# Key numbers of a product-key search by XOR and minimum on 16-bit numbers

## The reference, cut to what matters

```python
q = jnp.einsum('bsd,dk->bsk', h, w_q).reshape(b, s, PEER_HEADS, 2, PEER_DHALF)
sc = jnp.einsum('bshpk,hpnk->bshpn', q, sub_keys).astype(jnp.float32)
s1, i1 = lax.top_k(sc[..., 0, :], PEER_TOPK)       # 16 of 128
s2, i2 = lax.top_k(sc[..., 1, :], PEER_TOPK)
cand = (s1[..., :, None] + s2[..., None, :]).reshape(b, s, PEER_HEADS, PEER_TOPK * PEER_TOPK)
cidx = (i1[..., :, None] * PEER_N_KEYS + i2[..., None, :]).reshape(b, s, PEER_HEADS, PEER_TOPK * PEER_TOPK)
top, pos = lax.top_k(cand, PEER_TOPK)              # 16 of 256
idx = jnp.take_along_axis(cidx, pos, axis=-1)
gate = jax.nn.softmax(top, axis=-1)
```

## Time and profile before

| | us |
|---|---|
| runs (3): median | 4100.17 |
| lowest, highest | 4097.18, 4105.68 |
| profiled execution | 4106.96 |
| its span, first to last instruction | 4105.1 |
| granted clock of TensorE, mean | 0.953 of full speed |

### The profile page before, as it was taken

How to read it: one execution, slowest core, us unless ns; L and a number is a source line. 1 busy time by engine, 2 the same in 40 slices (tenths; PEclk the granted TensorE clock), 3 DMA queues, 4 the chain that set the end, 5 groups by cost and what they waited for, 6 DMA issues and landing times.

```text
span 4105.1 us, 46071 instructions
## 1 busy us (share of the span) xinstructions
PE 3706.4 (90%) x14431; PEld 2467.1 (60%) x14431; DVE 2709.5 (66%) x5504; ACT 1238.0 (30%) x2640; POOL 1580.5 (39%) x1341
## 2 busy tenths in 40 slices
PE   6999989898888979867769899798999999999998
PEld 5778768677777768656434454453544545445763
DVE  1445542348778866666999989889876868743540
ACT  1333332232333232225342240330422404224530
POOL 2556534331222147655344443443454444410000
PEclk8999999899999989988889999899999999999999
DMA  7666633347766658878899999999999999963557
GB/s 237 203 223 218 211 103 93 97 157 238 233 220 222 219 177 262 275 237 313 315 362 391 361 391 368 353 388 356 381 402 393 406 404 394 398 266 125 185 199 275
DMA packets 506183, 1133.96 MB, mean 276 GB/s; under 512 B 41036, under 2 KB 250364, under 8 KB 505760
## 3 DMA queue, kind: packets, MB, share of 16 engines
q1 hardware_dynamic: 334976, 570.93, 40.2%
q0 software_dynamic: 147456, 536.94, 35.0%
q10 hardware_dynamic: 23584, 24.12, 1.7%
HBM read 1044.80 MB, written 89.41 MB: 276 GB/s over the span
## 4 chain that ended last, share of the span: by engine, by line
PE 34%; DVE 14%; DMA 3%; issue 2%; ACT 1%; POOL 0%; DVEq 0%; ACTq 0%; SPq 0%
PE ps L1390 27%; DVE u_ring L2399 6%; PE ps L1376 4%; PE ps L1422 2%; DMA u_ring<-in_peer_u,pidx 1%; DMA v_ring<-in_peer_v 1%; DVE split_v L2446 1%; ACT split_v L1846 1%; DVE hot L2391 1%; DVE hot L2392 1%; DVE pick_own L2002 0%; DVE pick_own L1997 0%; DVE got_own L2005 0%; PE h_up L1365 0%; DVE inds_own L1960 0%
## 5 line engine op out<-in xcount | busy, mean ns | idle before, releaser
L1390 PE MATMUL ps<-v_ring,table 128*128 128x512 f32 x3584 | 1593.1, 596 | 16.6 <-DMA v_ring<-in_peer_v 16.6
L993 POOL DMA_INDIRECT u_ring<-in_peer_u,pidx x800 | 772.1, 965 | 969.8 <-DVE coefe L2399 902.0
L1390 PEld LDWEIGHTS ps<-v_ring,table 128*128 128x128 f32 x3584 | 664.1, 191 | 772.2 <-issue 723.7
L2399 DVE CUSTOM_DVE_ANT_0 u_ring<-u_ring,h_up 128x1024 f32<-128x1024 f32 x800 | 948.1, 1218 | 140.4 <-DMA u_ring<-in_peer_u,pidx 125.1
L1052 PE MATMUL ps<-x_hi,w_hi 128*128 128x512 f32 x1280 | 516.1, 403 | 39.7 <-ACT w_hi L1498 23.6
L1055 PE MATMUL ps<-x_lo,w_hi 128*128 128x512 f32 x1280 | 506.0, 395 | 0.0
L937 POOL TENSOR_TENSOR w_lo<-w_raw,w_hi 128x1024 fp32r<-128x1024 f32 x120 | 302.1, 2522 | 196.5 <-ACT w_hi L1498 190.7
L1376 PEld LDWEIGHTS ps<-hot,hot 128*128 128x128 f32 x2048 | 282.0, 203 | 155.2 <-issue 112.6
L1814 ACT ACTIVATE table<-ps 128x512 f32<-128x512 f32 (+3 forms) x256 | 229.5, 896 | 438.4 <-PE ps L1376 391.7
L958 POOL DMA_INDIRECT e_ring<-in_peer_u,icole x224 | 233.7, 1043 | 290.4 <-DVE dotse L2057 210.9
L1802 ACT ACTIVATE hot<-hot,by_slot 128x128 f32<-128x128 f32 x1024 | 322.3, 389 | 73.4 <-DVE hot L2391 51.6
(11 more groups left out here) (332 smaller groups left out, 4266.5 us busy)
## 6 DMA issues: line engine op xcount, KB each, us to landing
v_ring<-in_peer_v SPq DMA_DIRECT2D x576, 512.0 KB
w_raw<-in_w_in SPq DMA_DIRECT2D x88, 512.0 KB
wh_d<-w_hi SPq DMA_DIRECT2D x56, 512.0 KB, 2.7
wl_d<-w_lo SPq DMA_DIRECT2D x56, 512.0 KB, 4.2
w_hi<-wh_d SPq DMA_DIRECT2D x56, 512.0 KB
w_lo<-wl_d SPq DMA_DIRECT2D x56, 512.0 KB
u_ring<-in_peer_u,pidx POOLq DMA_INDIRECT x800
raw_mid<-in_w_branch SPq DMA_DIRECT2D x48, 256.0 KB
```

The lines of the kernel that those rows point to most:

```text
L993: pool.indirect_dma_start(out=u_ring[:, slot_of(n, k), :], out_offset=None, in_=u_tab, in_offset=bass.IndirectOffsetOnAxis(ap=pidx[n % 2][ ...
L1390: last = pe.matmul(ps[2 * (n % 2) + c][:, :], table[:, row_of(n, i1), :], v_ring[:, j % V_TILES, HALF * c:HALF * c + HALF], start=(n == p ...
L2399: dve.tensor_tensor_reduce(out=u_ring[:, slot_of(n, k), :], in0=u_ring[:, slot_of(n, k), :], in1=h1_up[:, :, :].rearrange("p c n -> p (c n)"),
```

## The change

In part 1 the indices are no longer converted: 128 times the place (0 to 15) is added to them, with a constant `steps` that is loaded at the start, into 16-bit numbers `indk`. In part 3 the position's high and low four bits are shifted to the same place (times 128) and written twice each into `own`. The XOR of `indk` and `own` is the index alone, under 128, where the places agree, and 128 or more elsewhere; so the minimum along the 16 is the wanted index. The conversion `posf`, the comparison and the product go. `pick`, `indk` and `own` are 16-bit tiles at the places of the tiles before them; `steps` takes 64 bytes per partition ahead of most other tiles.

```diff
+        "c_steps": np.tile(np.arange(TOPK, dtype=np.uint32) * P, (P, 1)),
...
+        steps = at("steps", [P, TOPK], U32)
...
+            sp.dma_start(steps[:, :], A["c_steps"]).then_inc(const_in, 16)
...
-            pe.wait_ge(const_in, 176)
+            pe.wait_ge(const_in, 192)
...
-            dve.wait_ge(const_in, 176)
+            dve.wait_ge(const_in, 192)
...
-                    dve.tensor_copy(tk.indf[:, :, :], tk.inds[:, :, :]).then_inc(*mark("indf"))
+                    dve.tensor_tensor(out=tk.indk[:, :, :], in0=tk.inds[:, :, :], in1=steps[:, :].unsqueeze(1).to_broadcast([P, 4, TOPK]),
+                                      op=ALU.add).then_inc(*mark("indf"))
...
-                    dve.tensor_scalar(out=tk.posu[:, :, 0, :], in0=tk.pos[:, :, :], scalar1=4, scalar2=None, op0=ALU.logical_shift_right).then_inc(*mark("pos1_"))
-                    dve.tensor_scalar(out=tk.posu[:, :, 1, :], in0=tk.pos[:, :, :], scalar1=TOPK - 1, scalar2=None, op0=ALU.bitwise_and).then_inc(*mark("pos2_"))
-                    md("pos2_")
-                    dve.tensor_copy(tk.posf[:, :, :, :], tk.posu[:, :, :, :]).then_inc(*mark("posf"))
-                    md("posf")
-
-                    dve.tensor_tensor(out=tk.pick[:, :, :], in0=tk.iota[:, :].unsqueeze(1).to_broadcast([P, 4 * TOPK, TOPK]),
-                                      in1=tk.posf[:, :, :, :].rearrange("p h t k -> p (h t k)").unsqueeze(2).to_broadcast([P, 4 * TOPK, TOPK]),
-                                      op=ALU.is_equal).then_inc(*mark("eq"))
-                    md("eq")
-                    pk = tk.pick[:, :, :].rearrange("p (m k) c -> p m k c", m=4)
-                    dve.tensor_tensor(out=pk, in0=pk, in1=tk.indf[:, :, :].unsqueeze(2).to_broadcast([P, 4, TOPK, TOPK]),
-                                      op=ALU.mult).then_inc(*mark("in"))
-                    md("in")
-                    dve.tensor_reduce(out=tk.got[:, :, :, :].rearrange("p h t k -> p (h t k)"), in_=tk.pick[:, :, :], axis=AX, op=ALU.add).then_inc(*mark("got"))
+                    places = tk.pos[:, :, :].bitcast(U16).rearrange("p h (k w) -> p h k w", w=2)[:, :, :, 0:1].to_broadcast([P, 2, TOPK, 2])
+                    dve.tensor_scalar(out=tk.own[:, :, 0, :, :], in0=places, scalar1=TOPK * (TOPK - 1), scalar2=3,
+                                      op0=ALU.bitwise_and, op1=ALU.logical_shift_left).then_inc(*mark("own1_"))
+                    dve.tensor_scalar(out=tk.own[:, :, 1, :, :], in0=places, scalar1=TOPK - 1, scalar2=7,
+                                      op0=ALU.bitwise_and, op1=ALU.logical_shift_left).then_inc(*mark("own2_"))
+                    md("own2_")
+
+                    four = [P, 4, TOPK, TOPK // 2, 2]
+                    dve.tensor_tensor(out=tk.pick[:, :, :].rearrange("p (m k) (c u) -> p m k c u", m=4, u=2),
+                                      in0=tk.indk[:, :, :].unsqueeze(2).to_broadcast([P, 4, TOPK, TOPK]).rearrange("p m k (c u) -> p m k c u", u=2),
+                                      in1=tk.own[:, :, :, :, :].rearrange("p h t k u -> p (h t) k u").unsqueeze(3).to_broadcast(four),
+                                      op=ALU.bitwise_xor).then_inc(*mark("off"))
+                    md("off")
+                    dve.tensor_reduce(out=tk.got[:, :, :, :].rearrange("p h t k -> p (h t k)"), in_=tk.pick[:, :, :], axis=AX, op=ALU.min).then_inc(*mark("got"))
```

More of the change, by code:

```diff
@@ L30 @@
 U32 = mybir.dt.uint32
+U16 = mybir.dt.uint16
 ALU = mybir.AluOpType
@@ L317, in layer @@
         inds_side = at("inds_side", [P, 4, TOPK], U32)
-        indf_side = at("indf_side", [P, 4, TOPK])
+        at("indf_side", [P, 4, TOPK])
         got_side = at("got_side", [P, 2, 2, TOPK])
@@ L356, in early_topk_tiles @@
             t.cleft = at("cleft_all", [P, 2, TOPK * TOPK])
-            t.pick = at("pick_all", [P, 4 * TOPK, TOPK], offset=where["ptp1"] + 2048)
-            t.iota = keys[:, 0:TOPK]
+            t.pick = nc.alloc_sbuf_tensor_at("pick_all", [P, 4 * TOPK, TOPK], U16, offset=where["ptp1"] + 2048)
             t.vals = at("vals_all", [P, 4, TOPK], offset=where["chain"] + 2048)
             t.inds = at("inds_all", [P, 4, TOPK], U32)
-            t.indf = at("indf_all", [P, 4, TOPK])
-            t.posu = at("posu_all", [P, 2, 2, TOPK], U32)
-            t.posf = at("posf_all", [P, 2, 2, TOPK])
+            at("indf_all", [P, 4, TOPK])
+            t.indk = nc.alloc_sbuf_tensor_at("indk_all", [P, 4, TOPK], U16, offset=where["indf_all"])
+            at("own_all_", [P, 2, 2, TOPK])
+            t.own = nc.alloc_sbuf_tensor_at("own_all", [P, 2, 2, TOPK, 2], U16, offset=where["own_all_"])
             t.got = at("got_all", [P, 2, 2, TOPK])
@@ L377, in side_topk_tiles @@
             t.cleft = at("cleft_side", [P, 2, TOPK * TOPK])
[L378 to L381, removed]
+            t.pick = nc.alloc_sbuf_tensor_at("pick_side", [P, 4 * TOPK, TOPK], U16, offset=where["w_raw1"])
+            t.vals, t.got, t.best, t.pos = vals_side, got_side, best_side, pos_side
+            t.indk = nc.alloc_sbuf_tensor_at("indk_side", [P, 4, TOPK], U16, offset=where["indf_side"])
             t.inds = inds_side
-            t.posu = at("posu_side", [P, 2, 2, TOPK], U32, offset=where["inds_side"])
+            t.own = nc.alloc_sbuf_tensor_at("own_side", [P, 2, 2, TOPK, 2], U16, offset=where["inds_side"])
             return t
@@ L449, in late_topk_tiles @@
             t.cleft = lay("cleft", "hot1_1", 0, [P, 2, TOPK * TOPK])
-            t.pick = lay("pick", "hot1_0", 0, [P, 4 * TOPK, TOPK])
-            t.iota = keys[:, 0:TOPK]
+            t.pick = lay("pick", "hot1_0", 0, [P, 4 * TOPK, TOPK], U16)
             t.vals = lay("vals", "hot2_0", 1024, [P, 4, TOPK])
-            t.posf = lay("posf", "hot2_0", 1024, [P, 2, 2, TOPK])
             t.inds = lay("inds", "hot2_0", 1280, [P, 4, TOPK], U32)
-            t.posu = lay("posu", "hot2_0", 1280, [P, 2, 2, TOPK], U32)
-            t.indf = lay("indf", "hot2_0", 1536, [P, 4, TOPK])
+            t.own = lay("own", "hot2_0", 1280, [P, 2, 2, TOPK, 2], U16)
+            t.indk = lay("indk", "hot2_0", 1536, [P, 4, TOPK], U16)
             t.got = lay("got", "hot2_0", 1792, [P, 2, 2, TOPK])
@@ L516, in layer @@
         TA = Steps(sem("topk_act"), ["ex"])
-        TK = Steps(sem("topk_dve"), "max at rest max2 at2 indf cand cmax cat crest cmax2 cat2 pos1_ pos2_ posf eq in got idx gsub".split())
+        TK = Steps(sem("topk_dve"), "max at rest max2 at2 indf cand cmax cat crest cmax2 cat2 own1_ own2_ off got idx gsub".split())
         TG = Steps(sem("gates_dve"), "gsum grec gate".split())
```

## The result

The changed kernel takes 4052.8 us, the median of four runs (4048.3 to 4059.0); the kernel before, run beside it, 4102.9 (4097.2 to 4106.3). The ratio is 0.9878, 95% interval 0.9861 to 0.9895: 50.1 us less by the medians, between 43 and 57 by the interval. The forecast was 4053.5. The profiled execution took 4052.45 us, its span 4050.6.

What follows compares the result with a forecast made beforehand. DVE was taken to set the end of passes 0 to 3 and the pace of the heads from `gm` to `ho1`. 31.4 − 1.0 + 16.8 − 0.5 = 46.7 us off 4100.2 gave 4053.5 us; range 4046 to 4062, 8 in 10 4044 to 4072.

Steps and rivals of the forecast that it cites:

- The cost of one search: In each of the 32 searches on DVE, the new lookup saves 1.96 us, or 1.42 with the XOR at four-byte rate.
- the lower end for the XOR: In part 3 of a search, the two-byte XOR takes 0.69 us, not 1.225, as its operands lie in adjacent pairs.
- rival 1: In every search, the XOR runs no faster than four-byte numbers: 34.2 us saved, 4066.0 us; chance 0.19.
- Late: 16 searches in passes 0 to 3, where DVE sets the end: 7.84 us a pass, 31.4 us in all.
- The 1.0 us taken off for pass 1: In pass 1, the gather near its highest rate takes back 1.0 us, between nothing and 2.
- It fits, barely: In pass 1, the gather's bytes need 106.1 us at the highest rate; the shortened pass would have 108.3.
- Heads: 12 searches beside the second half's heads: two of three pay 1.96 us each, 3.92 us a head.
- The first head: Of the 1.96 us by which DVE starts earlier after the fourth early search, 1.15 remain when `gm` meets ScalarE's sigmoid.
- The constant: At the start, one more DMA load in front of nine that DVE and PE wait for costs 0.5 us, once.
- Rivals 2: The heads give nothing, or the gather halves the saving of passes 1 to 3: 4065 to 4071 us; chance 0.10.
- Rival 3: In the searches, the XOR falls under the four-byte rate, 3.3 us for 1024 elements: slower, 4116 us; chance 0.03.
- rival 4: Better: the minimum is paired too, 4041 us, or PE's clock rises sooner, 1 to 2 us; chance 0.03.

Runs made afterwards that it cites:

- E6: Changed kernel with the XOR of the first search of each head done five times over: 4066.5 us, ratio 0.9907 to the kernel before.
- E4: Changed kernel with two-byte numbers kept but no pairs, the XOR repeating a single number 16 times: 4066.3 us, ratio 0.9905 to the kernel before.
- E8: Changed kernel with the XOR of each late search done five times over: 4100.7 us, ratio 0.9986 to the kernel before.
- E9: Changed kernel without the XOR and the minimum, one operation over 64 elements in their place: 4028.6 us, ratio 0.9821 to the kernel before.
- E7: Changed kernel with the XOR of the third search of each head done five times over: 4054.9 us, ratio 0.9877 to the kernel before.
- E3: Kernel before with the new lookup only in the 12 searches beside the heads, and the constant: 4085.4 us, ratio 0.9947.
- E1: Kernel before with the new constant alone, its 64 bytes a partition and its load, no search changed: 4101.8 us, ratio 0.9989.
- E5: Kernel before with the 64 bytes a partition kept free in the layout and nothing loaded: 4102.0 us, ratio 0.9991.
- E12: Changed kernel with four-byte whole numbers throughout the lookup: 4063.1 us, ratio 0.9894 to the kernel before.

## Why the prediction was right

*The cost of one search.* 1.96 us forecast, 4.30 − 2.31 = 1.99 from `own1` to `idx`, less 0.03 for `indk` (225 ns for 196): 1.96. Each term stood: XOR 693 ns for 0.69 taken, with the late ones at 710 on average in the changed kernel (691 to 749) and 693 in E6; minimum 1220 ns; `own` 190 ns each. The choice that decided was the lower end for the XOR. It was argued from 16 ns for 32 more elements of a conversion, a thin row; E4 shows how near the other end was: the same operation, types and count, 1225 ns, and rival 1 with it. It also bears out the reason that the forecast gave, that the operands are laid in pairs: without them nothing is left of the saving of the XOR.

*Late.* DVE sets the end of passes 0 to 3, 30.4 us (4 × 7.84 less 1.0): the stages gave 30.8, E8 gave the slope, 44.3 for 46. The 1.0 us taken off for pass 1 did not show (7.5 us saved there), nor did DVE wait noticeably longer for rows (10.9 us in the pass, 10.5 before). "It fits, barely" was right in another sense: PE's gap there fell to 3.12 us, and E9 found no microsecond more there.

*Heads.* Two of three searches pay. E6 against E7 is that claim for the first and the third, 11.9 us and nothing for the same 11.5 us of work, and DVE's timeline has the second: from `vt0` to `ho1` the four heads take 7.7 us less for 7.84 forecast, in E3 7.5, in E8 6.2. From `gm` to `ho1` it is 15.4 us less for 15.7, in E3 and E8 13.7. The stage as a whole gave 16.8 for 14.9 to 15.7; the part above is within the scatter of the stretches that PE paces. PE's wait for `v_tmp` is 2.65 us a head for 2.3 forecast, DVE's for `cmc` 4.0 for 4.6. At L1176 PE's wait fell by 3.0 us (13.2 to 10.2) where the reasoning has 7.8. So that wait is a poor measure of what the second search gives; the stretch of DVE that ends at `ho1` is the better one.

*The first head.* 1.15 us was to be left of the fourth early search (the two times that the prediction names for it lie 1.18 apart). Its `idx` is 7.48 us ahead of before in the changed kernel, of which the stretch since `o_hi` is 1.83. The first `hg` after it is only 958.46 − 952.19 = 6.27 ahead, held by ScalarE:

```profile
952.19 0.69 DVE L2099 TENSOR_TENSOR hg<-ps,hg 128x512 f32<-128x512 f32 x1 [3.48 <-ACT hg L1556]
```

So about 0.6 us was left, half of the term.

*The constant.* This is the step that failed: −0.5 us was taken, and E1 and E5 say +4, though neither is far from nothing. It is the only term of the wrong sign. By stages the searches give 30.8 + 16.8 + 2.0 = 49.6 us, for 31.4 − 1.0 + 16.8 = 47.2 forecast; with the layout's share 53.6. The 50.1 measured, with an interval from 43 to 57, agrees with either, and with the forecast of 46.7. So the timing confirms the sum, but it can't tell a layout's share from none.

*What the rivals were.* Rival 1 is real as a size (E4, E12), not as the case. Rivals 2 and 3 are out. Rival 3 was also priced from a misread row: the eight instructions `he1n` of the earlier trace rows are products, and their 1766 ns is the mean of four of the first half at 2840 to 2855 ns, with POOL at work beside them, and four of the second at 683 to 687. No instruction of that group took 1.77 us.

Of rival 4, the minimum isn't paired as a reduction (1220 ns in all types here). Its other half, the clock, shows in the heads. Windows over the heads (length, busy of PE, PEld, DVE, ACT, POOL, PEclk, DMA, GB/s), before and changed:

```profile
943.01:1494.85 551.84, 478.39 (x2356) 401.63 (x2354) 424.36 (x1163) 168.08 (x368) 124.16 (x122) 0.92 0.66 214
```

```profile
935.53:1472.36 536.83, 472.27 (x2365) 397.67 (x2363) 401.15 (x1139) 169.66 (x370) 120.21 (x122) 0.93 0.68 221
```

PE was busy 6.1 us less there with the same work (478.1 to 479.5 us in the five traces with the old lookup, 467.9 to 473.9 in the three with the new), at a granted clock of 0.93 for 0.92, and 11.7 us less over the whole span (3706.4 to 3694.7, clock 0.953 to 0.958). What of this reaches the end of the kernel, no run separates.

## What to carry to other kernels

Where an engine sets the end, its saving counts in full only until the next resource is met; read the gap left behind it, and the resource's rate, before spending on a second step: 2 us a search paid in full here, the next 1.7 us by little more than half (23.4 of 42). In a stretch where two engines take turns, find for each piece of work which wait comes behind it: the same work was worth 12 us ahead of PE's wait and nothing ahead of DVE's own. Two-byte operands are worth laying out in pairs, since the type alone changed nothing.

## What was not expected of the hardware

A two-byte XOR of 1024 elements took 1225 ns when one operand repeats a single half-word, and 693 ns when it repeats a pair; in four bytes it was 1224 ns. A reduction took 1220 ns in float32 (a sum), uint32 and uint16 (minima) alike, while a two-byte `tensor_tensor` minimum of 512 took 425. And 64 bytes a partition, unused, went with a kernel some 4 us faster before any of the changed code ran, which isn't settled.
